# Neighbourhood attention with maps turned in squares and placed through DRAM

## What is computed

```python
q, k, v, g = split(h @ w_in, 4)            # 16 heads of 64, 256 tokens = 4 rows of 64
kc, vc = split(hc @ w_in[:, 1024:3072], 2) # 256 context tokens
s_loc = q @ k.T + bias[row difference, column difference]  # 16 columns around the query
s_ctx = q @ kc.T
p = softmax(concat(s_loc, s_ctx))          # 256 + 256 keys
o = p_loc @ v + p_ctx @ vc
y = (o * silu(g)) @ w_out                  # [256, 1024]
x = x + gate * y
# second network, mixing, one branch of it:
s = q @ k.T * scale + rel_bias[:, clip(query - key)]
```

## Time and profile before

| | |
|---|---|
| median of 3 runs | 1814.81 us (1814.69 to 1815.71) |
| profiled execution, its own time | 1815.61 us |
| its span | 1813.8 us |
| TensorE busy | 1793.3 us (99%) |
| weight loads / VectorE / ScalarE / GpSimd busy | 1477.5 / 954.2 / 901.5 / 1366.0 us |
| TensorE's mean granted clock | 0.998 of full speed |
| DMA moved | 372.91 MB, mean 206 GB/s |
| attention loop (scores of unit 0 to the end of step 15) | 303.9 to 370.6 us |
| convolution layer's input blocks | from about 398 us |

### The profile page before, as it was taken

One profiled execution on the slowest core, in us unless ns is written; L12 is line 12 of the kernel. 1 busy time (PEld: TensorE's weight loads), 2 busy tenths in 40 slices (PEclk: granted clock), 3 DMA queues, 4 the chain that ended last, 5 costly groups with the idle time before them and its releaser, 6 DMA issues.

```text
span 1813.8 us, 24988 instructions
## 1 busy us (share of the span) xinstructions
PE 1793.3 (99%) x9274; PEld 1477.5 (81%) x9274; DVE 954.2 (53%) x1756; ACT 901.5 (50%) x1329; POOL 1366.0 (75%) x568
## 2 busy tenths in 40 slices
PE   6999999999999999999999999999999999999999
PEld 5888888887889888887788888888888878888887
DVE  4673766778755524866653230713095876143152
ACT  3324424674455644456554644464445565555452
POOL 2624544559968898977689798969897867888885
PEclk9999999999999999999999999999999999999999
DMA  9863885749775775565665566567655666656663
GB/s 366 291 210 94 270 310 163 198 141 312 244 277 200 211 221 191 180 198 168 209 186 192 179 195 191 193 187 234 191 193 185 192 190 182 196 160 210 190 195 128
DMA packets 206457, 372.91 MB, mean 206 GB/s; under 512 B 33508, under 2 KB 59092, under 8 KB 205780
## 3 DMA queue, kind: packets, MB, share of 16 engines
q1 hardware_dynamic: 203328, 363.69, 63.5%
q10 hardware_dynamic: 3028, 7.86, 1.2%
HBM read 367.27 MB, written 9.28 MB: 208 GB/s over the span
## 4 chain that ended last, share of the span: by engine, by line
PE 97%; DVE 2%; DMA 0%; issue 0%; ACTq 0%; ACT 0%; POOL 0%; DVEq 0%
PE ps L1300 26%; PE ps L1302 25%; PE ps L1301 25%; PE ps L1426 3%; PE ps L1427 3%; PE ps L1428 3%; PE ps L1992 1%; PE ps L1993 1%; PE ps L1994 1%; PE ps L1348 1%; PE ps L1697 1%; PE ps L1918 1%; PE ps L1668 1%; PE ps L1678 1%; PE ps L1962 1%; PE ps L1558 1%
## 5 line engine op out<-in xcount | busy, mean ns | idle before, releaser
L659 POOL TENSOR_TENSOR w_lo<-raw,w_hi 128x1024 fp32r<-128x1024 f32 x556 | 1347.1, 2461 | 397.4 <-ACT w_hi L697 376.2
L1300 PE MATMUL ps<-w_hi,act_rows_r 128*128 128x512 f32 x2064 | 814.8, 395 | 3.2 <-POOL w_lo L659 3.1
L1302 PE MATMUL ps<-w_hi,act_rows_r 128*128 128x512 f32 x2064 | 805.2, 390 | 0.0
L1301 PE MATMUL ps<-w_lo,act_rows_r 128*128 128x512 f32 x2064 | 804.6, 390 | 0.0
L697 ACT ACTIVATE w_hi<-raw 128x1024 fp32r<-128x1024 f32 x556 | 571.1, 1058 | 371.0 <-DMA raw<-in_ffn_w_up 100.8
L1300 PEld LDWEIGHTS ps<-w_hi,act_rows_r 128*128 128x128 f32 x2064 | 388.2, 188 | 90.4 <-issue 9.1
L1302 PEld LDWEIGHTS ps<-w_hi,act_rows_r 128*128 128x128 f32 x2064 | 388.0, 188 | 82.0
L1301 PEld LDWEIGHTS ps<-w_lo,act_rows_r 128*128 128x128 f32 x2064 | 388.4, 188 | 77.7
L2647 DVE STREAM_TRANSPOSE ps<-proj 32x256 f32<-32x256 f32 (+1 forms) x384 | 166.5, 434 | 6.5
L2628 DVE TENSOR_TENSOR proj<-proj,ps 128x1024 f32<-128x1024 f32 (+1 forms) x18 | 20.4, 1132 | 252.2 <-PE ps L1302 247.9
L1426 PE MATMUL ps<-act_rows_r,w_hi 128*128 128x512 f32 (+1 forms) x288 | 101.3, 352 | 0.0
(11 more groups left out here) (245 smaller groups left out, 1554.0 us busy)
## 6 DMA issues: line engine op xcount, KB each, us to landing
raw<-in_w_in SPq DMA_DIRECT2D x120, 512.0 KB, 3.9
raw<-in_ffn_w_gate SPq DMA_DIRECT2D x88, 512.0 KB, 4.4
raw<-in_ffn_w_up SPq DMA_DIRECT2D x88, 512.0 KB, 4.4
raw<-in_ffn_w_down SPq DMA_DIRECT2D x88, 512.0 KB, 4.2
proj<-in_ada_w SPq DMA_DIRECT2D x39, 512.0 KB, 7.9
pt<-in_ada_w SPq DMA_DIRECT2D x38, 512.0 KB, 6.4
raw<-in_pool_w_in SPq DMA_DIRECT2D x32, 512.0 KB, 7.3
raw<-in_na_w_in SPq DMA_DIRECT2D x32, 512.0 KB, 4.9
```

The source lines that it names most:

```text
L659: pool.tensor_tensor(w_lo[:, s, :], raw[:, s, :], w_hi[:, s, :].bitcast(F32), ALU.subtract).then_inc(lo_done, 1)
L1300: pe.matmul(o, h, hi, start=start, stop=False)
L1301: pe.matmul(o, h, lo, start=False, stop=False)
L1302: return pe.matmul(o, c, hi, start=False, stop=stop)
```

## The change

- Units 0, 2, 4, 6, 8 and 10 (`NA_SQUARED`) are no longer transposed by TensorE. VectorE transposes their exponents in 32x32 squares, one instruction of 128x1024; SyncE writes the result to DRAM (`keep_squares`) and reads it back into place by four DMAs (`place_squares`). TensorE multiplies from there, five steps after the scores in place of three (`na_due`). There are two places in DRAM and one in SBUF.
- ScalarE scales gate quarters 0 and 1, as it does quarter 3, in steps 10 and 11; VectorE halves the reciprocals after units 3 and 7 too. Quarter 2 stays on VectorE.
- A head pair's bias comes by four DMAs of 876-byte rows into a buffer of its own; GpSimd takes windows of it and adds the mask into `bias`, in two instructions. The load waits for the mask two pairs before; GpSimd waits for the logits. The first two pairs load after group 12 of `na_in` in place of 7.
- The relation copy of layer 0 goes behind group 12 of `cv_in`, that of layer 1 into the second feed-forward of layer 0.

```diff
+NA_SQUARED = (0, 2, 4, 6, 8, 10)
...
 def na_out_bank(u):
-    return 2 if u < NA_UNITS - 3 else 4
+    return 3 if u == NA_SQUARED[-1] else 2 if u < NA_UNITS - 3 else 4
+def na_due(i):
+    return [u for u in range(NA_UNITS - 1) if u + (5 if u in NA_SQUARED else 3) == i]
+def na_last_of(k):
+    return 4 * k + 2 if 4 * k + 2 in NA_SQUARED else 4 * k + 3
+def na_placed_rows(dims, at=0, rows=slice(0, P)):
+    return free(proj[rows, 0:1], dims, CTX_RES + 2 * D + at)
+def bias_windows(hp, dims, at=0, rows=slice(0, P)):
+    return free(proj[rows, 0:1], dims, CTX_RES + D + (hp % 2) * 512 + at)
 def na_rows_of(u, dims, at=0):
...
 def load_bias(hp):
-    for h, t, rq in ((h, t, rq) for h in range(2) for t in range(NT) for rq in range(2)):
-        src = bass.AP(na_rows.tensor, (2 * hp + h) * RPB_HEAD + (7 - 2 * t - rq) * RPB_C + 15,
-                      [[NA_ROW - 1, GRID_W], [RPB_C, 4], [1, GRID_W]])
-        sp.dma_start(free(bias[64 * rq:64 * rq + 64, 0:1], [[64, 4], [1, GRID_W]],
-                          (hp % 2) * 1024 + h * 512 + t * 256), src).then_inc(bias_in[hp % 2], 16)
+    if hp >= 2:
+        sp.wait_ge(bias_masked, hp - 1)
+    for h in range(2):
+        for rq in range(2):
+            src = bass.AP(na_rows.tensor, (2 * hp + h) * RPB_HEAD + (5 - rq) * RPB_C + 15, [[NA_ROW - 1, GRID_W], [1, RPB_SPAN]])
+            sp.dma_start(bias_windows(hp, [[1, RPB_SPAN]], h * 256, slice(64 * rq, 64 * rq + 64)), src).then_inc(bias_in[hp % 2], 16)
 def keep_map(l, i):
...
-    if prev == "p0_out":
-        sp.wait_ge(scratch_in, 16)
-        load_bias(0)
-        load_bias(1)
+if stage == "na_in" and g == 12:
+    sp.wait_ge(scratch_in, 16)
+    load_bias(0)
+    load_bias(1)
+if stage == "cv_in" and g == 12:
+    keep_rel(0)
...
+def keep_squares(u):
+    sp.wait_ge(dve_done, dve_s.count(("na_sq", u)))
+    if u >= 4:
+        sp.wait_ge(na_placed, 64 * (u // 2 - 1))
+    sp.dma_start(na_squares[u // 2 % 2], bias[:, 2048:3072]).then_inc(na_kept, 16)
+def place_squares(u):
+    sp.wait_ge(na_kept, 16 * (u // 2 + 1))
+    if u:
+        sp.wait_ge(pe_done, pe_s.count(("na_out", u - 2)))
+    for kq in range(4):
+        sp.dma_start(na_placed_rows([[256, 4], [1, 256]], 0, slice(32 * kq, 32 * kq + 32)),
+                     bass.AP(na_squares.tensor, u // 2 % 2 * P * 1024 + 256 * kq, [[1024, 32], [32 * 1024, 4], [1, 256]])).then_inc(na_placed, 16)
 def keep_gates(l):
...
+    squared = 2 * j - 2 in NA_SQUARED
-        sp.wait_ge(dve_done, dve_s.count(("na_l", 2 * j + 1)))
+    if squared:
+        keep_squares(2 * j - 2)
-    if j in (1, 3):
-        keep_rel(j // 2)
+    if squared:
+        place_squares(2 * j - 2)
+sp.wait_ge(na_kept, 16 * len(NA_SQUARED))
...
-def ffn_weights(gate, up, down, tables=False):
+def ffn_weights(gate, up, down, tables=False, copied=None):
+        if pair == 2 and copied is not None:
+            keep_rel(copied)
...
 def masked(hp):
-    pool.wait_ge(bias_in[hp % 2], 128 * (hp // 2 + 1))
-    both = free(bias[:, 0:1], [[SEQ, 4], [1, SEQ]], (hp % 2) * 1024)
-    pool.tensor_tensor(both, both, free(na_mask[:, 0:1], [[0, 4], [1, SEQ]]), ALU.add).then_inc(bias_masked, 1)
+    pool.wait_ge(bias_in[hp % 2], 64 * (hp // 2 + 1))
+    if hp >= 2:
+        pool.wait_ge(dve_done, dve_s.count(("na_l", 2 * hp - 3)))
+    for t in range(NT):
+        last = pool.tensor_tensor(free(bias[:, 0:1], [[512, 2], [GRID_W, 4], [1, GRID_W]], (hp % 2) * 1024 + t * SEQ),
+                                  bias_windows(hp, [[256, 2], [RPB_C, 4], [1, GRID_W]], 2 * RPB_C * (1 - t)),
+                                  free(na_mask[:, 0:1], [[0, 2], [GRID_W, 4], [1, GRID_W]]), ALU.add)
+    last.then_inc(bias_masked, 1)
...
+def gate_scaled(k):
+    act.wait_ge(dve_done, dve_s.count(("na_half", k)))
+    b = B0["na_in"] + 6 + k // 2
+    act.wait_ge(acc_free[b % 2], reads(b))
+    for t in range(NT):
+        for h in range(4):
+            v = pj(3 * D + k * SEQ + h * HD, HD, NA_COLS, t=t)
+            r = NA_INV + 8 * k + 4 * t + h
+            last = act.activation(v, v, ACT.Copy, scale=rstat[:, r:r + 1])
+    last.then_inc(act_done, act_s.one(("na_g", k)))
-        if i >= 3:
+        if i - 3 in NA_SQUARED:
+            act.wait_ge(dve_done, dve_s.count(("na_sq", i - 3)))
+        elif i >= 3:
...
-act.wait_ge(dve_done, dve_s.count(("na_half", 3)))
-act.wait_ge(acc_free[(B0["na_in"] + 7) % 2], reads(B0["na_in"] + 7))
-for t in range(NT):
-    for h in range(4):
-        v = pj(4 * D - SEQ + h * HD, HD, NA_COLS, t=t)
-        r = NA_INV + 24 + 4 * t + h
-        last = act.activation(v, v, ACT.Copy, scale=rstat[:, r:r + 1])
-last.then_inc(act_done, act_s.one(("na_g", 3)))
+gate_scaled(3)
...
 def na_values(u):
-    pe.wait_ge(dve_done, dve_s.count(("na_pt", u, 0)))
-    pe.wait_ge(act_done, act_s.count(("na_pt", u, 1)))
+    if u in NA_SQUARED:
+        pe.wait_ge(na_placed, 64 * (u // 2 + 1))
+    else:
+        pe.wait_ge(dve_done, dve_s.count(("na_pt", u, 0)))
+        pe.wait_ge(act_done, act_s.count(("na_pt", u, 1)))
...
-last = pe.matmul(ps[c * HD:(c + 1) * HD, bank, 0:P], v, pt[:, o:o + P], start=k == 0, stop=k == 3)
+maps = na_placed_rows([[256, 4], [1, 32]], 32 * (4 * c + k)) if u in NA_SQUARED else pt[:, o:o + P]
+last = pe.matmul(ps[c * HD:(c + 1) * HD, bank, 0:P], v, maps, start=k == 0, stop=k == 3)
...
-if i >= 2:
+due = na_due(i)
+for u in due[:-1]:
+    na_values(u)
+if i >= 2 and i - 2 not in NA_SQUARED:
-if i >= 3:
-    na_values(i - 3)
+for u in due[-1:]:
+    na_values(u)
...
 def turned(u):
-    dve.wait_ge(pe_done, pe_s.count(("na_t", u, 0)))
-    if u >= 2:
-        dve.wait_ge(pe_done, pe_s.count(("na_out", u - 2)))
-    dve.tensor_copy(pt[:, (u % 2) * 1024:(u % 2) * 1024 + 512], ps[:, 6, :]).then_inc(dve_done, dve_s.one(("na_pt", u, 0)))
+    if u in NA_SQUARED:
+        dve.wait_ge(act_done, act_s.count(("na_e", u, 1)))
+        if u:
+            dve.wait_ge(na_kept, 16 * (u // 2))
+        dve.transpose(free(bias[:, 0:1], [[32, 8], [256, 4], [1, 32]], 2048),
+                      na_rows_of(u, [[P, 8], [32, 4], [1, 32]])).then_inc(dve_done, dve_s.one(("na_sq", u)))
+    else:
+        dve.wait_ge(pe_done, pe_s.count(("na_t", u, 0)))
+        if u >= 2 and u - 2 not in NA_SQUARED:
+            dve.wait_ge(pe_done, pe_s.count(("na_out", u - 2)))
+        dve.tensor_copy(pt[:, (u % 2) * 1024:(u % 2) * 1024 + 512], ps[:, 6, :]).then_inc(dve_done, dve_s.one(("na_pt", u, 0)))
-    if u == NA_UNITS - 1:
+    if u in (3, 7, NA_UNITS - 1):
-        r = rstat[:, NA_INV + 24:NA_INV + 32]
-        dve.tensor_scalar(r, r, 0.5, None, ALU.mult).then_inc(dve_done, dve_s.one(("na_half", 3)))
+        r = rstat[:, NA_INV + u // 4 * 8:NA_INV + u // 4 * 8 + 8]
+        dve.tensor_scalar(r, r, 0.5, None, ALU.mult).then_inc(dve_done, dve_s.one(("na_half", u // 4)))
 def gate_made(n):
...
-if i in (10, 12):
-    gate_scaled((i - 10) // 2)
+due = na_due(i)
+for u in due[:-1]:
+    values(u)
-if i >= 3:
-    values(i - 3)
+for u in due[-1:]:
+    values(u)
```

More of the change, by code:

```diff
@@ L23 @@
 RPB_HEAD = 15 * RPB_C
+RPB_SPAN = 5 * RPB_C + GRID_W
 LAYERS = 2
@@ L174, in program @@
     map_rows = nc.dram_tensor("map_rows", (2, P, 768), F32, kind="Internal").ap()
+    na_squares = nc.dram_tensor("na_squares", (2, P, 1024), F32, kind="Internal").ap()
     gate_scratch = nc.dram_tensor("gate_scratch", (DEPTH, KC, 2, P), F32, kind="Internal").ap()
@@ L235, in program @@
         decay_in = sem("decay_in")
+        na_kept, na_placed = sem("na_kept"), sem("na_placed")
         maps_kept, maps_in = ([sem(f"{n}{k}") for k in range(2)] for n in ("maps_kept", "maps_in"))
@@ L559, in tables_of @@
                     send_table(mix_cols[:, 6:7], bass.AP(I["a_subln_2"].tensor, l * 128, [[1, P], [1, 1]]))
-                    if l == 0:
-                        sp.wait_ge(rel_in, 16 * 2 * LAYERS)
+                    sp.wait_ge(rel_in, 32 * (l + 1))
                     send_table(free(bias[:, 0:1], [[P, 8], [1, P]], 0), bass.AP(rel_rows.tensor, l * P * REL_PITCH + 256,
@@ L639, in _ @@
                 wide(I["w_out_2"][l], 8)
-                ffn_weights(I["ffn2_w_gate_2"][l], I["ffn2_w_up_2"][l], I["ffn2_w_down_2"][l])
+                ffn_weights(I["ffn2_w_gate_2"][l], I["ffn2_w_up_2"][l], I["ffn2_w_down_2"][l],
+                            copied=l + 1 if l + 1 < LAYERS else None)
             assert sent[0] == GROUPS
@@ L958, in na_layer @@
                         na_gate(6 + i // 8)
+                    if i in (10, 11):
+                        gate_scaled(i - 10)
                     if i == NA_UNITS:
@@ L962, in na_layer @@
                         u = i - 2
-                        act.wait_ge(pe_done, pe_s.count(("na_t", u, 1)))
-                        if u >= 2:
-                            act.wait_ge(pe_done, pe_s.count(("na_out", u - 2)))
-                        act.activation(pt[:, (u % 2) * 1024 + 512:(u % 2) * 1024 + 1024], ps[:, 7, :],
-                                       ACT.Copy).then_inc(act_done, act_s.one(("na_pt", u, 1)))
```

(12 more changed lines are left out.)

## The result

Six runs of the changed kernel have a median of **1820.88 us** (1815.10 to 1823.62), six of the kernel before 1815.16 (1814.69 to 1815.71): ratio 1.0027, 95% interval 1.0017 to 1.0038. The forecast was 1812.5, range 1809.3 to 1817.0: it was wrong, in size and in sign. In two later sittings the same kernel had 1815.66 (ratio 1.0010, 1.0001 to 1.0019) and 1816.42 (1.0014, 1.0003 to 1.0024): slower each time, by an amount that differs between sittings.

A forecast was written before the change was run, and what follows sets the result against it. TensorE, busy for 99% of the span, was taken as the bound. Terms -5.2 + 1.0 + 0.4 - 0.25 + 0.4 + 1.3 = -2.35 us, from 1815.6 and less 0.8, gave 1812.5 us; range 1809.3 to 1817.

The forecast's parts named there:

- Transposes off TensorE: Attention loop: six units lose their eight transposes on TensorE, 0.87 us each time, -5.2 us.
- about 4: Sign to look for in the changed kernel: an attention loop about 4 us shorter.
- The loop's start: First units of the attention loop: TensorE waits 0.48 us before scores 3 and 0.55 before scores 4, +1.0 us.
- Maps through DRAM: Attention loop: value products wait on transposing, write and four reads; SyncE 7.4 us per pair against TensorE's 7.9; +0.4 us.
- rival 3: Attention loop: SyncE's queue becomes the bound, units 2, 4, 6, 8 each 2.25 us late; 1821.1 us, chance 0.11.
- Bias: Attention loop, unit 8: the late mask that delayed logits and scores 9 goes, -0.25 us.
- gate quarters: Units 10 and 11: quarters 0 and 1 on ScalarE, 2.01 us each, delay unit 12's copy; +0.4 us, bounds 0 and 1.6.
- Rival 4: Units 10 and 11: ScalarE's multiplications count wholly, 2 x 2.01 us in place of 0.4; 1816.0 us, chance 0.05.
- Relation copy: Convolution, behind group 12: copy delays later loads by 4.5 us against 3.2 of room; TensorE waits, +1.3 us, bounds 0 and 5.5.
- Rival 2: Convolution: the relation copy takes 8.7 us, costing 5.5 in place of 1.3; 1816.7 us, chance 0.09.
- Rival 1: Convolution and attention loop: the relation copy and the placed maps are both hidden; 1810.8 us, faster, chance 0.33.
- Idle time in a feed-forward stage: Sign that the prediction is wrong altogether: idle time appearing in a feed-forward stage, where the moved copy was charged nothing.

## Why the prediction was wrong, step by step

- *Transposes off TensorE, -5.2.* Right: 80 transposes for 128, 48 matmuls fewer on the page, and in executions without map waits the stage is 4.02 us shorter, near the "about 4".
- *The loop's start, +1.0.* 0.7 of it: scores 4 waited 0.49 (forecast 0.55), by the chain that was worked out; scores 3 did not wait, a turn ahead of them did, 0.19.
- *Maps through DRAM, +0.4, bounds 0 and 9.* Mis-sized: 1.9, 0 and 0.4 us in three profiles of the changed kernel, 1.2 to 2.1 in four kernels with six units. The ring was summed to 7.4 us against TensorE's 7.9; it took 8.1, 8.7 and 9.3 in the first profile and 7.6 to 8.1 in the one without a wait. The half microsecond of room is less than the spread of a landing (2.6 to 4.0 us), and the write stood behind the bias loads. So this is rival 3's place at a fifth of its price, varying from run to run. Write first alone left 1.6 us; with unit 0 left out as well it is 0.
- *Bias -0.25, gate quarters +0.4.* Together 0 without squares (94.36 against 94.37), and in the changed kernel no scores of units 12 and 13 wait for logits. Rival 4 falls: with the squares there, ScalarE's 2.01 us a quarter is the better place by 0.45 to 0.8 us in the profile. The Trainium skill ("ScalarE: Activation LUTs", section "Rules for kernel authors") gives multiplications to VectorE. In this case's profiles the engine that is slower when alone (2.01 us against 0.75) was the better place.
- *Relation copy, +1.3.* **The step that failed.** Its form, the copy's delay X less the room, held; its numbers did not. X was taken as 4.5, and the room of 3.2 was read at load 20 and TensorE's group 17. Load 19 was the one hit, and TensorE waited for its add-up: it landed 7.0 us later after its issue (12.5 against 5.5), less some 1.4 us of room at VectorE, which waited 5.57, less 2.8 at TensorE, which waited 2.74. So delay and room were both taken too small, by 2.5 and 1.1 us; that the two errors cancel in part is luck. And after the wait TensorE ran at the lower clock level for 3.4 us, a price of 1.7 us that no term held. 2.7 + 1.7 = 4.4, and with the 0.35 below it makes 4.8 of the 4.85. Rival 2 had 5.5 for the wait, 0.09 for its chance, and no clock either.
- *Not in the sum*: 0.35 us at the convolution's second turn, where TensorE, earlier than before, waits 0.3 us for VectorE's normalised rows. It is in every profile with squares and the gates on ScalarE, and not in the one with the gates back. And the 0.33 us outside the span, which the prediction took as 1.8 us on both sides.
- *Sum.* Rival 1, both hidden, falls. In the third sitting's profile, with map waits of 0.4, the two stages and the 0.33 give -3.5 + 4.0 + 0.33 = +0.8 us, near the 0.8 and 1.5 us of the two later sittings. The 5.7 of the first is not accounted for: its profile, without the luck of the start, gives -1.96 + 4.85 - 0.05 + 0.33 = +3.2, and no execution above 1820 was profiled. That its median lies near rival 3's 1821.1 says nothing for rival 3: the profile has 1.9 us of map waits, not 9.

"Idle time in a feed-forward stage" would have made it wrong altogether: there was none (1367.07 against 1367.12 from the third add-up to the end).

## What to carry to other kernels

Price a transfer put into a full DMA stretch by the *next* load that an engine waits for, and add the clock: a wait of TensorE of 2 us cost 3.7 here, while half the transfer cost nothing. A ring of write, reads and consumer that fits by half a microsecond in the sum does not fit, since its landings spread by more; here the write first in its queue and the first turn dropped made it fit together. A gain of 4 us in one place and a loss of 4 to 5 in another look like "no change": split the change before judging any part of it.

## What the runs showed of the hardware

- TensorE's clock fell from 2.4 to 1.2 GHz after waits of 1.9, 2.0, 2.1, 2.74 and 2.78 us in otherwise full stretches, each time for 3.4 us; it stayed at 2.4 GHz after waits of 0.96, 1.0 and 1.47 us.
- VectorE's multiplications of two operands took longer while GpSimd worked: a gate quarter 1.74 and 2.10 us beside the mask and 0.75 beside an idle GpSimd; one multiplication of 128x512 7.32, 2.68 and 1.38 us beside low halves and 0.69 after them. No run varies GpSimd's work alone.
- A copy of 1.5 MB from DRAM to DRAM ahead of a load, with the DMA engines full, made that load's landing 12.5 us instead of 5.5 after issue; half the copy made it 7.4.
- The same program in three sittings had medians of 1820.9, 1815.7 and 1816.4, while the kernel before stayed within 1814.9 to 1815.2.
